# Six gate chunks moved into an earlier decode stage, dilated softmax sums taken from the exponentials and swapped as turned rows, and half of the experts' down projection split into high and low parts

## The chip, the cores and the metric

The kernel runs on one core of one Trainium2 chip. The metric is device time in microseconds (us) of one launch; three runs of the kernel before gave 2228.87, 2231.35 and 2236.27 us, median 2231.35 us.

## The reference, cut to what matters

One layer of a decoder for 1024 prompt tokens and 8 sample tokens (one for each of 8 sequences with 256 cached positions), model width 1024, fp32:

```
u = rmsnorm(h);  z = u @ W_in          # q,k,v of 12 dilated and 8 stick-breaking heads, gates g_a and g_b
h += ( sigmoid(g_a) * (dilated(u) @ W_oa) + sigmoid(g_b) * (stick(u) @ W_ob) ) @ W_out
h += experts(rmsnorm(h))               # 32 experts, 2 for each token: (silu(x @ Wg) * (x @ Wu)) @ Wd
h += sigmoid(rmsnorm(h) @ W_pg) * (p @ W_pp);   y = rmsnorm(h)
```

Dilated attention has three groups of four heads: windows 128, 512 and 2048 with strides 1, 4 and 16. The three groups of one head position are joined by a softmax over their log-sums, which is one softmax over all their keys: all exponentials take one common maximum for each query and are divided by one common sum. Stick-breaking attention takes a reverse running sum of softplus over the keys. For the sample tokens both kinds read cached keys and values (the stick-breaking ones from pages named by a table).

## The kernel before, in words

The kernel is a chain of stages, each a block that all engines enter and leave together: norm and projection, `stick_and_gates` (L368), `dilated` (L672), `decode` (L970), merge, residual, routing, `experts` (L1761), finish.

Matmuls that go by `products` (L83 to L89) split both fp32 operands into a high part (a ScalarE copy to fp32r) and a low part (a VectorE subtraction) and make three one-pass products: high by low, low by high, high by high. Other matmuls are plain fp32; the trace has two instructions for each.

`stick_and_gates`: 64 units (4 head pairs, 8 query tiles in the order 7,0,6,1,5,2,4,3, 2 heads) go through a pipeline written out by hand: step s scores one part (ScalarE copies it out), masks unit s-1, exponentiates s-2, scans s-3 (VectorE), s-4 exponentials, turns s-5 on TensorE, s-6 values, s-7 out. Between these TensorE is given matmuls of the two output gates, shared out evenly over the steps: 16 chunks of 128 columns, each 3 groups of 344 tokens by 24 products, 1152 in all (`gates`, L545). Each chunk is loaded by SP (L474), split by ScalarE (L569) and VectorE (L626), and goes out to DRAM as `gT`.

`dilated`: two head pairs. A pair has 16 units of 128 queries: units 0 to 7 are the stride-1 group with natural rows of queries, units 8 to 15 the other two groups with queries in classes modulo 4. Scores run 18 steps ahead of the exponentials (between the pairs 4 more steps), since the maxima of the two orders have to be joined: SP writes the maxima of units 0 to 7 to DRAM element by element (L795), reads them back by classes (L798), writes those of units 8 to 15 (L801) and reads them back in natural order (L804); VectorE joins them (L927, L929). Then for each unit: exponential (ScalarE L900), turn on TensorE (L843) and copies out (ScalarE L893, VectorE L935), values (TensorE L867) twice, once with V and once with a tile of ones, which gives the sums, and eviction of both (ScalarE L886 for units 0 to 7, VectorE L960 adds for 8 to 15). At the end of a pair VectorE takes the reciprocal of 128x1024 sums (L964) and multiplies (L966).

`decode`: scores of the 8 sample tokens on VectorE (multiply and reduce over loaded keys, L1153, L1177, L1181), softmax or the stick-breaking chain on 32 or 64 rows, then values: a row of all heads is made (L1260, L1266), masked to each head's own columns on VectorE (L1199, L1203) and turned by products with ones (L1274). The pages of keys and then of values go into one buffer (`KV` is `big`), so the value pages are loaded only after all key products (L1070). TensorE has nothing else to do in this stage.

`experts`: 32 blocks of 128 rows, two for each pass of a loop, software-pipelined: in a step TensorE makes the gate of block n-1, turns the hidden rows of n-2, makes up of n-1, turns the rows of n, and makes down of n-2 (L1891, plain fp32, 4 parts of the hidden width by 2 halves of the output). ScalarE order: output of n-3, sigmoid of n-1, high parts of Wg, x, Wu of n. VectorE order: gated n-1, copy of the turned hidden rows n-2, low parts of Wg, hidden n-1, low parts of x and Wu. Each block loads 6 MB of weights and 0.5 MB of rows and stores 0.5 MB.

Of the kernel before, what the change touches and what calls it, by code (L numbers as in the profile page):

```python
# [19 lines left out]
P = 128  # L20
D = 1024
# [30 lines left out]
NEG = -1.0e30  # L52
SCALE = HD ** -0.5
# [314 lines left out]
def stick_and_gates(nc, g):  # L368
# [5 lines left out]
    with ctx:  # L374
# [10 lines left out]
        CH = 2 * KD  # L385
# [12 lines left out]
        gw = sb("g_w", [P, KD, P])  # L398
        gwh = sb("g_wh", [P, 2, KD, P], F32R)
        gwl = sb("g_wl", [P, 2, KD, P], F32R)  # L400
# [4 lines left out]
        acc = [ps(f"g_acc{j}", [P, 512]) for j in range(2)]  # L405
# [6 lines left out]
        gw_in = sem("g_w_in")  # L412
        g_out = [sem(f"g_g_out{j}") for j in range(2)]
        gwh_full, gwl_full, acc_full, gate_full = map(sem, ("g_wh_full", "g_wl_full", "g_acc_full", "g_gate_full"))
# [48 lines left out]
        def _(sp):  # L463
# [8 lines left out]
            def load_gate(c):  # L472
                need(sp, gwl_full, c)
                sp.dma_start(gw[:, :, :], win_v[:, :, QKV + c * P:QKV + (c + 1) * P]).then_inc(gw_in, 16)  # L474
# [7 lines left out]
            for s in range(LAST + 1):  # L482
# [8 lines left out]
                for c in range(CH):  # L491
                    if evict_at[c * NSPLIT + NSPLIT - 1] == s:
                        sp.wait_ge(gate_full, (c + 1) * NSPLIT)
                        sp.dma_start(gT[c, :, :], gate[:, c % 2, :]).then_inc(g_out[c % 2], 16)
            for b in range(2):
                sp.wait_ge(g_out[b], 16 * CH // 2)
# [175 lines left out]
def dilated(nc, g):  # L672
# [6 lines left out]
    with ctx:  # L679
# [12 lines left out]
        EXP_LAG, TURN_LAG, VALUE_LAG, EVICT_LAG = 18, 19, 20, 21  # L692
# [24 lines left out]
        def keys(u, x, m):  # L717
# [9 lines left out]
        LAST = max(at_evict) + 1  # L727
# [7 lines left out]
        acc = sb("acc", [P, PAIRS, 2, SEQ])  # L735
        ones = sb("ones", [P, HD])
        mst = sb("mst", [P, PAIRS, 2, UNITS])
        oth = sb("oth", [P, PAIRS, 2, UNITS])
        nm = sb("nm", [P, PAIRS, 2, UNITS])
# [6 lines left out]
        O = [ps(f"O{n}", [P, 512]) for n in range(2)]  # L746
        drawn, kept, bias_step, bias_set = map(sem, ("drawn", "kept", "bias_step", "bias_set"))
        s_full, row_full, joint_step, nm_full, p_full, tp_full, o_full, oa_read, ob_read, fin = map(sem, (
            "s_full", "row_full", "joint_step", "nm_full", "p_full", "tp_full", "o_full", "oa_read",
            "ob_read", "fin"))  # L750
        pT_full = [sem(f"pT_full{b}") for b in range(2)]
# [3 lines left out]
        m_in = [sem(f"m_in{p_}") for p_ in range(PAIRS)]  # L755
# [4 lines left out]
        def nat(p_, n):  # L760
            return maxes[p_, n, :, :].rearrange("b (i p) -> p b i", p=P)
# [4 lines left out]
        by_class = lambda t, p_: t[:, p_, :, QT:UNITS].rearrange("p b (h r) -> p b h r", h=2)  # L766

        @block.sync
        def _(sp):
            def load_qk(p_, x):  # L770
                c = x * PAIRS + p_
# [1620 lines left out]
```

## Time and profile before

| what | value |
|---|---|
| median of three runs | 2231.35 us |
| the profiled execution: device time, span | 2228.89 us, 2227.3 us |
| TensorE busy, VectorE, ScalarE, GpSimd | 1855.4, 1057.1, 800.7, 128.4 us |
| mean granted TensorE clock | 0.911 |
| DMA moved | 401.73 MB, mean 180 GB/s |
| stick_and_gates | 443 to 787 us |
| dilated | 787 to 984.6 us |
| decode | 984.6 to 1108 us |
| experts | 1403 to 2041 us |

The span is the time from the first to the last instruction; the device time of the same execution lies 1.6 us above it. Busy shares are of the whole span; what counts is the stage. A granted clock of 1.00 is 2.4 GHz and 0.50 is 1.2 GHz.

### The profile page before, as it was taken

How to read it: one execution, taken by the hardware profiler on the slowest of the kernel's cores; microseconds unless marked ns; L12 is line 12 of the kernel's file. 1: busy time of each engine (PE TensorE's matmuls, PEld its weight loads, DVE VectorE, ACT ScalarE, POOL GpSimd, SP SyncE). 2: the span in 40 equal slices, each digit the busy share in tenths (PEclk: the TensorE clock that was granted, in tenths of full speed). 3: DMA queues.
4: the chain of work that ended last, by engine and by line, in shares of the span. 5: the costliest groups of instructions: out<-in, count | busy, mean ns of one | idle time of the engine just before them, and what ended most of it. 6: DMA issues, size and time to landing. Idle time of an engine off the chain costs nothing. (4 is left out here: it accounts for less than half of the span.)

```text
span 2227.3 us, 26881 instructions
## 1 busy us (share of the span) xinstructions
PE 1855.4 (83%) x9852; PEld 1443.3 (65%) x9852; DVE 1057.1 (47%) x1415; ACT 800.7 (36%) x1096; POOL 128.4 (6%) x181
## 2 busy tenths in 40 slices
PE   5999999789999947632498992599999999996698
PEld 4999999777777835431295541466666677773585
DVE  5211211158888733335151224466666666662674
ACT  4111111147666503220040000454555555452454
POOL 0111111100000000010031003000000000001110
PEclk7999999989999978675699995699999999998799
DMA  3443444245221160025354213899999999994620
GB/s 114 116 121 114 131 126 122 92 140 172 67 86 39 39 180 1 1 55 152 99 167 145 76 39 137 354 390 379 381 384 385 382 385 382 382 378 164 224 75 39
DMA packets 165325, 401.73 MB, mean 180 GB/s; under 512 B 25659, under 2 KB 102955, under 8 KB 144772
## 3 DMA queue, kind: packets, MB, share of 16 engines
q1 hardware_dynamic: 146004, 334.32, 41.8%
q0 software_dynamic: 10320, 33.82, 5.3%
q10 hardware_dynamic: 8928, 32.63, 3.6%
q8 instruction: 45, 0.74, 0.1%
q14 instruction: 28, 0.23, 0.0%
HBM read 325.80 MB, written 82.61 MB: 183 GB/s over the span
## 5 line engine op out<-in xcount | busy, mean ns | idle before, releaser
L87 PE MATMUL p_acc<-uh,p_wl 128*128 128x344 f32 x720 | 234.9, 326 | 13.0 <-DVE ul L293 9.0
L89 PE MATMUL p_acc<-uh,p_wh 128*128 128x344 f32 x720 | 230.6, 320 | 0.0
L88 PE MATMUL p_acc<-ul,p_wh 128*128 128x344 f32 x720 | 230.5, 320 | 0.0
L1891 PE MATMUL x_Y<-x_wd,x_hT 128*128 128x512 f32 x512 | 225.1, 593 | 0.8 <-DVE x_hT L1989 0.8
L305 DVE COPY p_zk<-p_tp 128x512 f32<-128x512 f32 (+1 forms) x90 | 44.2, 547 | 304.4 <-PE p_tp L226 304.4
L1973 DVE TENSOR_TENSOR x_wgl<-x_wg,x_wgh 128x2048 fp32r<-128x2048 f32 x64 | 143.9, 2290 | 49.8 <-ACT x_wgh L1930 49.8
L1891 PEld LDWEIGHTS x_Y<-x_wd,x_hT 128*128 128x128 f32 x512 | 95.0, 190 | 108.2 <-issue 107.1
L269 ACT ACTIVATE p_zc<-p_acc 128x344 f32<-128x344 f32 x90 | 41.2, 458 | 321.6 <-PE p_acc L89 321.6
L1973 DVE TENSOR_TENSOR x_wul<-x_wu,x_wuh 128x2048 fp32r<-128x2048 f32 x64 | 143.8, 2289 | 17.8 <-ACT x_wuh L1930 17.8
L87 PEld LDWEIGHTS p_acc<-uh,p_wl 128*128 128x128 f32 x720 | 135.8, 189 | 18.0 <-issue 14.9
L545 PE MATMUL g_acc<-uh,g_wl 128*128 128x344 f32 x384 | 129.1, 336 | 9.3 <-ACT u L576 7.1
L89 PEld LDWEIGHTS p_acc<-uh,p_wh 128*128 128x128 f32 x720 | 136.0, 189 | 0.0
L88 PEld LDWEIGHTS p_acc<-ul,p_wh 128*128 128x128 f32 x720 | 135.8, 189 | 0.0
L1930 ACT ACTIVATE x_wgh<-x_wg 128x2048 fp32r<-128x2048 f32 x64 | 118.8, 1905 | 47.2 <-DMA x_wg<-in_w_gate 47.2
L1505 PE MATMUL r_acc<-r_w,mT 128*128 128x512 f32 (+1 forms) x288 | 127.3, 601 | 10.1 <-DMA r_w<-in_w_out 10.1
L545 PE MATMUL g_acc<-ul,g_wh 128*128 128x344 f32 x384 | 127.4, 332 | 0.0
L545 PE MATMUL g_acc<-uh,g_wh 128*128 128x344 f32 x384 | 126.9, 330 | 0.0
L87 PE MATMUL x_G<-x_wgh,x_xl 128*128 128x512 f32 x256 | 114.0, 445 | 11.5 <-DVE x_xl L1967 11.5
L1930 ACT ACTIVATE x_wuh<-x_wu 128x2048 fp32r<-128x2048 f32 x64 | 118.5, 1901 | 0.3 <-DMA x_wu<-in_w_up 0.3
L1978 DVE TENSOR_TENSOR x_gs<-x_sg,x_G 128x512 f32<-128x512 f32 x32 | 22.1, 689 | 178.6 <-ACT x_sg L1923 178.6
L1505 PEld LDWEIGHTS r_acc<-r_w,mT 128*128 128x128 f32 (+1 forms) x288 | 51.6, 182 | 79.6 <-issue 69.2
L87 PE MATMUL x_U<-x_wuh,x_xl 128*128 128x512 f32 x256 | 102.9, 402 | 0.0
(316 smaller groups left out, 3676.8 us busy)
## 6 DMA issues: line engine op xcount, KB each, us to landing
x_wg<-in_w_gate SPq DMA_DIRECT2D x64, 1024.0 KB, 7.7
x_wu<-in_w_up SPq DMA_DIRECT2D x64, 1024.0 KB, 7.4
x_wd<-in_w_down SPq DMA_DIRECT2D x32, 2048.0 KB, 12.5
x_x<-xs SPq DMA_DIRECT2D x32, 512.0 KB, 11.6
ys<-x_y ACTq DMA_DIRECT2D x32, 512.0 KB, 11.8
zT<-p_zc ACTq DMA_DIRECT2D x30, 516.0 KB, 3.4
p_w<-in_w_in SPq DMA_DIRECT2D x30, 512.0 KB, 5.5
ztok<-p_zk POOLq DMA_DIRECT2D x30, 512.0 KB, 4.6
```

The costliest lines, as they stand in the source:

```text
L87: pe.matmul(out, w_low, m_high, start=first, stop=False)
L88: pe.matmul(out, w_high, m_low, start=False, stop=False)
L89: return pe.matmul(out, w_high, m_high, start=False, stop=last)
L269: act.activation(zc[:, b, s * NS:(s + 1) * NS], acc[b * NSPLIT + s][:, 0:NS], ACT.Copy).then_inc(zc_full, 1)
L305: dve.tensor_copy(zk[0:r, b, t0:t0 + m, :], tp[j % 2][0:r, 0:m, :]).then_inc(zk_full, 1)
L545: last = pe.matmul(acc[grp % 2][:, 0:NS], lhs[:, c % 2, kk, :], rhs[:, kk, t], start=(x == 0), stop=(x == M - 1), skip_group_check=True)
L1505: last = pe.matmul(acc[t % 2][0:r, c * 512:(c + 1) * 512], mT[:, k, t * P:t * P + r], w[:, k, c * 512:(c + 1) * 512], start=(k == 0), stop ...
L1891: last = pe.matmul(Y[c][:, :], hT[:, k, :], wd[:, b, k, c * 512:(c + 1) * 512], start=(k == 0), stop=(k == KF - 1))
L1930: act.activation(wh[:, HALVES[half], :], w[:, HALVES[half], :], ACT.Copy).then_inc(full, 1)
L1973: dve.tensor_tensor(wl[:, s, :], w[:, s, :], wh[:, s, :], ALU.subtract).then_inc(full, 1)
L1978: dve.tensor_tensor(gs[:, :], sg[:, :], G[:, :], ALU.mult).then_inc(gs_full, 1)
```

## The change

1. `decode` becomes `decode_and_gates` and runs before `stick_and_gates`. Its TensorE program has 20 steps, and in 18 of them it makes one group (24 products) of the first 6 gate chunks, the decode work standing ahead of the group in its step. The gate loads are issued by ScalarE. Key pages get a buffer of their own; value pages share the buffer of the dilated keys and queries and wait for `scored`. Values are made turned at once: V or the value page is the stationary operand and the weights of all heads the moving one, and a mask and a sum (`own_heads`) keep each head's own rows.
2. `stick_and_gates` makes the other 10 chunks (720 products), shared out over the same steps.
3. `dilated` drops the products with ones. Each exponential gives its row sums (`accum_out`). Maxima and sums change order as rows: natural ones are turned on TensorE to 16 rows of 128 and written in one piece. The natural maxima leave during the scoring. After the last exponential of a pair the class sums go by DRAM to natural rows, are turned and added, the reciprocal is taken of 128x16 values, turned, written, and read back broadcast to all partitions. The loads of V and of the second pair's q and k are issued by ScalarE.
4. `experts` splits two of the four hidden parts of the down projection into high and low parts (ScalarE and VectorE) and makes three products of each; the other two stay plain fp32.

The core of the diff:

```diff
+DECODE_GATES = 6
-            stick_and_gates(nc, g)
+            decode_and_gates(nc, g, DECODE_GATES)
+            stick_and_gates(nc, g, DECODE_GATES)
...
             dilated(nc, g)
-            decode(nc, g)
@@ stick_and_gates
-        CH = 2 * KD
+        CH = 2 * KD - c0
@@ dilated, TensorE
-                for side in range(2):
-                    for n, (x, t) in enumerate(tiles):
-                        for b in range(2):
-                            left = ones[:, :] if side else v[:, p_, x, t, h]
+                for n, (x, t) in enumerate(tiles):
+                    for b in range(2):
+                        last = pe.matmul(O[a % 2][h, 0:P], v[:, p_, x, t, h], pT[:, a % 2, b, n * P:(n + 1) * P], ...)
@@ dilated, ScalarE
+            act.wait_ge(qk_in[0][1], 32)
+            load_v(act, 0)
+            for x in range(N_DIL):
+                load_qk(act, 1, x)
+            load_v(act, 1)
...
-                        act.activation(r, r, ACT.Exp, scale=SCALE, bias=nm[:, p_, b, u:u + 1]).then_inc(p_full, 1)
+                        act.activation(r, r, ACT.Exp, scale=SCALE, bias=one(nm, p_, b, u),
+                                       accum_out=one(den, p_, b, u)).then_inc(p_full, 1)
@@ dilated, SP
+                for p_ in range(PAIRS):
+                    natural_out(p_)
+                    sp.wait_ge(row_full, 2 * (p_ + 1) * UNITS)
+                    classes_out(p_, mst, 1, mrows[:, p_, 1, :], m_out[p_][1], m_in[p_][1])
+                for p_ in range(PAIRS):
+                    sp.wait_ge(p_full, 2 * (p_ + 1) * UNITS)
+                    classes_out(p_, den, 2, drows[:, p_, 0, :], n_out[p_][0], n_in[p_][0])
+                    sp.wait_ge(inv_kept, p_ + 1)
+                    sp.dma_start(natural(p_, 3), drows[:, p_, 1, :]).then_inc(n_out[p_][1], 16)
+                    sp.wait_ge(n_out[p_][1], 16)
+                    for b in range(2):
+                        sp.dma_start(inv[b * HD:(b + 1) * HD, p_, :], maxes[p_, 3, b, :]...broadcast_to([HD, SEQ]))
@@ decode_and_gates
+        D_SCORES_T, D_PROBS_T, D_VALUES = 6, 7, 8
+        S_SCORES_T, S_WEIGHTS_T, S_VALUES = 13, 14, 16
+        STEPS = GROUPS + 2
+        S_SCORES = {9: (0, 1), 10: (1, 3), 11: (3, 5), 12: (5, 8)}
+        cut_at = {max(0, (c - 1) * NSPLIT): c for c in range(1, chunks)}
...
+            def outputs_T(o, rows_, weights, heads, b0, b1):
+                for b in range(b0, b1):
+                    for c in range(o.shape[1]):
+                        for x in range(2):
+                            last = pe.matmul(o[:, c, b, :], rows_(x, b)[:, c * P:(c + 1) * P],
+                                             weights[:, x, b * heads:(b + 1) * heads], ...)
@@ experts
             def down(n, b, it):
+                    if k < KS:
+                        pe.wait_ge(dl_full, n * KS + (k + 1))
...
+                        if k < KS:
+                            last = products(pe, Y[c][:, :], hh[:, k, :], hl[:, k, :], wdh[:, k, cols], wdl[:, k, cols],
+                                            k == 0, False)
@@ experts, ScalarE step
                 if three:
                     output(*three)
+                if two:
+                    high_down(*two)
                 if one:
                     sigmoid(one[0])
+                if two:
+                    high_hidden(two[0])
@@ experts, VectorE step
+                if two:
+                    low_down(two[0], two[1])
                 if one:
                     gated(one[0])
@@ experts, ScalarE end
                 output(last - 1, 0, np_ - 1)
+                high_down(last, 1, np_ - 1)
+                high_hidden(last)
                 output(last, 1, np_ - 1)
```

## Rows read from the trace of the kernel before

**Rows 1.** Windows, by stage: start:end, us, busy by engine, granted clock, DMA share, GB/s
```profile
443.00:787.00 344.00, 308.98 (x2208) 257.95 (x2208) 257.57 (x432) 208.50 (x385) 0.49 (x2) 0.98 0.28 91
787.00:984.60 197.60, 122.13 (x972) 91.14 (x972) 70.88 (x201) 46.72 (x112) 2.24 (x7) 0.73 0.18 49
984.60:1108.00 123.40, 43.24 (x168) 23.68 (x168) 40.79 (x55) 3.60 (x7) 10.41 (x32) 0.61 0.46 127
1403.00:2041.00 638.00, 619.83 (x2432) 432.94 (x2432) 387.16 (x256) 318.66 (x257) 0.00 (x0) 0.98 0.94 367
```

**Rows 2.** Windows inside stick_and_gates
```profile
475.00:755.00 280.00, 260.52 (x1881) 214.63 (x1882) 234.71 (x397) 185.49 (x346) 0.00 (x0) 1.00 0.28 90
595.00:635.00 40.00, 34.99 (x251) 28.32 (x249) 34.56 (x58) 25.61 (x48) 0.00 (x0) 1.00 0.15 53
```

**Rows 3.** Timeline of stick_and_gates (start us, us): gate products, early and later
```profile
456.25 0.49 PE L545 MATMUL g_acc<-uh,g_wh 128*128 128x344 f32 x1
...
600.05 0.32 PE L545 MATMUL g_acc<-uh,g_wl 128*128 128x344 f32 x1
600.21 0.32 PE L545 MATMUL g_acc<-ul,g_wh 128*128 128x344 f32 x1
```

**Rows 4.** Groups by line, 450 to 783 us: busy, mean ns, idle before
```profile
L626 DVE TENSOR_TENSOR g_wl<-g_w,g_wh 128x1024 fp32r<-128x1024 f32 x16 | 19.6, 1223 | 43.5 <-ACT g_wh L569 43.5
```

**Rows 5.** Groups by line and form, dilated
```profile
L867 PE MATMUL d_O<-d_pT,d_ones 128*64 128x128 f32 x312 | 31.3, 338 | 0.0
```

**Rows 6.** Timeline of dilated, from the last scores of pair 0 to its first exponential
```profile
811.51 3.80 SPq L795 DMA_DIRECT2D maxes<-d_mst  x2
812.52 0.68 DVE L952 CUSTOM_DVE_ANT_0 d_row<-d_bias,d_S 128x512 f32<-128x512 f32 x1
824.83 0.87 SPq L798 DMA_DIRECT2D d_oth<-maxes  x2
825.75 0.98 SPq L801 DMA_DIRECT2D maxes<-d_mst  x2
831.46 0.19 DVE L927 TENSOR_TENSOR d_oth<-d_oth,d_mst 128x32 f32<-128x32 f32 x1 [18.25 <-DMA d_oth<-maxes]
```

**Rows 7.** Timeline of dilated, between the pairs and at the end
```profile
913.10 6.55 DVE L964 RECIPROCAL d_acc<-d_acc 128x1024 f32<-128x1024 f32 x1
...
969.43 1.32 ACT L900 ACTIVATE d_row<-d_row,d_nm 128x512 f32<-128x512 f32 x2
983.13 1.22 DVE L966 TENSOR_TENSOR u<-d_acc 128x1024 f32<-128x1024 f32 x1
```

**Rows 8.** Window inside dilated
```profile
930.00:940.00 10.00, 8.52 (x58) 6.39 (x54) 1.27 (x3) 3.55 (x11) 0.00 (x0) 0.50 0.00 0
```

**Rows 9.** Timeline of decode: first scores, one of 8 key products, last products
```profile
1006.48 2.29 DVE L1153 TENSOR_TENSOR g_big<-g_big 128x2048 f32<-128x2048 f32 x1 [22.13 <-DMA g_big<-ztok]
1057.11 1.22 DVE L1177 TENSOR_TENSOR g_big<-g_big,e_wide 128x1024 f32<-128x1024 f32 x1
1058.36 1.28 DVE L1181 TENSOR_REDUCE e_s<-g_big 128x8 f32<-128x512 f32 x2
1097.00 10.03 PE L1274 MATMUL e_bank<-c_ones,e_wide 8*128 8x1 f32 x64 [0.77 <-DVE e_wide L1203]
```

**Rows 10.** Window inside experts
```profile
1580.00:1680.00 100.00, 100.00 (x401) 70.09 (x400) 64.11 (x44) 50.91 (x43) 0.00 (x0) 1.00 0.97 384
```

**Rows 11.** Timeline of experts: every third gate product, then the last down projections
```profile
1708.84 0.39 PE L87 MATMUL x_G<-x_wgh,x_xl 128*128 128x512 f32 x1
...
1709.52 0.39 PE L87 MATMUL x_G<-x_wgh,x_xl 128*128 128x512 f32 x1
...
2023.37 7.03 PE L1891 MATMUL x_Y<-x_wd,x_hT 128*128 128x512 f32 x16
2030.23 0.63 PE L1882 MATMUL x_tph<-ident,x_hm 128*128 128x128 f32 x4
```

**Rows 12.** DMA issues of the page: count, KB each, us to landing
```profile
x_wd<-in_w_down SPq DMA_DIRECT2D x32, 2048.0 KB, 12.5
```

More of the change, by code:

```diff
@@ L844, in turn, with evicted, bank_read, bank_free @@
                     last.then_inc(tp_full, 1)
-            def values(a):
+            def evicted(a):
+                e_, w = place(a)
+                if w < QT:
+                    pe.wait_ge(oa_read, e_ * QT + w + 1)
+                else:
+                    pe.wait_ge(ob_read, e_ * QT + w - QT + 1)
+            def bank_read(s):
+                for steps, done, per in ((at_nat, nat_kept, 1), (at_joint, joint_step, 2), (at_sum, total_step, 2),
+                                         (at_inv, inv_kept, 1)):
+                    need(pe, done, per * sum(t < s for t in steps))
+            def bank_free(s):
+                before = [a for t, a in at_value.items() if t <= s and a % 2 == 0]
+                if before:
+                    evicted(max(before))
+                bank_read(s)
+            def values(a, at_step):
                 p_, u = place(a)
@@ L1133, in _ @@
                 keep(bias[:, 1, h:h + 1], True, OWN + N_DIL, -NEG)
-            then(pool.memset(ones[:, :], 1.0))
-            then(pool.memset(head[:, :, :], 0.0))
-            then(pool.affine_select(out=head[:, :, :], in_=head[:, :, :], compare_op=ALU.not_equal, fill=1.0,
-                                    base=0, pattern=[[-1, H_B], [0, HD]], channel_multiplier=1))
+            then(pool.memset(own[:, :, :], 0.0))
+            for c in range(CB):
+                for half in range(2):
+                    then(pool.memset(own[half * HD:(half + 1) * HD, c, 2 * c + half:2 * c + half + 1], 1.0))
             pool.memset(mx[:, :], 0.0).then_inc(bias_set, 1)
@@ L1171, in dilated_softmax, with own_heads @@
                 dve.tensor_scalar(st[:, :, :], st[:, :, :], mx[:, 3:4], None, ALU.mult).then_inc(pn_full, 1)
+            def own_heads(dst, src, full, heads):
+                dve.wait_ge(full, 1)
+                n = src.shape[1]
+                m = masked[:, 0:n * DEC * heads].rearrange("p (c b h) -> p c b h", c=n, b=DEC)
+                for c in range(n):
+                    ins = dve.tensor_tensor(m[:, c, :, :], src[:, c, :, :],
+                                            own[:, c, 0:heads].unsqueeze(1).to_broadcast([P, DEC, heads]), ALU.mult)
+                    if c < n - 1:
+                        ins.then_inc(dve_step, 1)
+                        steps[0] += 1
+                    else:
+                        then(ins)
+                dve.tensor_reduce(dst, m, AX, ALU.add).then_inc(done, 1)
             def stick_scores(b):
@@ L1280, in _ @@
+            for n in range(STEPS):
+                if n == D_SCORES_T:
                     pe.wait_ge(s_full, 2)
@@ L1941, in step @@
             def step(it, j):
-                one, three = lag(it, j, 1), lag(it, j, 3)
+                one, two, three = lag(it, j, 1), lag(it, j, 2), lag(it, j, 3)
                 new = it * 2 + j
```

587 lines of the change are left out of this document (343 added, 244 removed).

## The prediction

> **What bounds the kernel now.** I began with the windows by stage [rows 1]. Nearly all of the change falls into four stages: stick_and_gates, 344 us; dilated, 198; decode, 123; experts, 638. The reader is to see that each has a limit of its own. In stick_and_gates TensorE is busy 309 of 344 us at a clock of 0.98. In decode it is busy 43 of 123, the hole into which work is moved. In dilated it is busy 122 of 198 at a mean clock of 0.73, and DMA stands still. In experts it is busy without a break in the steady part, while DMA is 0.97 busy [rows 10]. Then I looked inside the stages. In the steady part of stick_and_gates TensorE has 260.5 of 280 us and VectorE 234.7 [rows 2]: TensorE ends last, but VectorE is only a tenth behind. The timeline of dilated shows two holes made by the join of the maxima [rows 6, 7] and steps in which TensorE alternates between values, sums and turns [rows 5]. The timelines of decode and experts give the chains below [rows 9, 11].
>
> **1. stick_and_gates loses 6 of 16 chunks.** That is 6 x 72 = 432 products. At full clock one starts every 0.158 us [rows 3], so TensorE loses 68.3 us of work. VectorE loses 6 splits of 1.22 us [rows 4], 7.3 us, ScalarE less than 15 us, and it is not the bound at 185 of 280 us [rows 2]. In the 280 us window TensorE's share of the loss is about 58 us, so its need falls to 203, and VectorE's to 229: VectorE is late next. The stage can't win 68 us. Before, VectorE stood idle 45 us in this window. Its largest wait in the whole stage, 43.5 us for the high part of a gate chunk [rows 4], is partly the start, which stays; the rest of its waits come from TensorE being late and mostly go. Bounds for the window: no idle left, 229 (a gain of 51); all of it left, 274 (a gain of 6). I take 15 us of idle, 244, a gain of 36, since TensorE now has 40 us to spare and the pipeline lets it run about a step ahead, but the heavy and light units alternate. Behind the last unit, after the window, fewer products fill TensorE: 6 us more, bounds 0 and 8. Together -42 us, bounds -6 and -59.
>
> **2. decode takes the 6 chunks in.** TensorE's own time: the first gate product can't come earlier than in stick_and_gates, some 13 us after that stage began [rows 1, 3], since gate loads, both splits and table loads are the same; 18 groups, 68.3 us; values as 32 + 64 matmuls of two instructions, 192, at the 0.157 us of the old turned outputs, whose stationary side has the same 128 columns [rows 9], 30 us; turns and the end, 5 us. Sum 116, and with nothing late that is the lower bound less what warmer clock gives on the values, 108. What can be late: the scores of step 6 need keys and queries, which before were there 22 us after the stage began [rows 1, 9] and now share the DMA queues with the gate loads, the broadcast queries of the stick-breaking heads and the first pages. Take 30; VectorE then needs 4 x 2.3 us for both scores, 39, and TensorE would be at step 6 at 13 + 23 = 36: a stall of 3 to 5 us. The second: VectorE's split of chunk 4 stands ahead of the first key product of a page and waits for step 8 of TensorE, about 60; from there 8 sequences at 2.5 us [rows 9], 20 us, and two splits, 2.4, give 83, while TensorE reaches step 13 at about 75: 8 us. These two bring 116 to 128; the values at full clock give some 5 back: 123 us. The old stage took 123.4 [rows 1], so the edit comes out at 0. Bounds: 108 (-15) and, with keys 10 us later still and the value pages late by 5, 138 (+15). SP's queue holds keys, queries, pages, V, pages and value pages in one order; decode's 15.7 MB (127 GB/s x 123.4 us) and six gate loads of 0.5 MB, 19 MB, need 160 GB/s of DMA that is 0.46 busy at 127 [rows 1]: not the bound.
>
> **3. dilated.** (a) The first hole. The last scores of pair 0 end at 813.2; the join, on which the exponentials wait, comes at 831.5 [rows 6]. Of this 11.6 us are behind the element-wise write of natural maxima (issued 811.5, done 824.8). It leaves during scoring now. What stays is one round trip, 825.75 to 831.46, 5.7 us, plus a turn and one more VectorE instruction, 0.8: join at 819.7, gain 12 us. If the row write queues behind V loads until 818, 5 us less; the bounds are 7 and 13. (b) The second hole: the reciprocal at 913.1 takes 6.55 us, the multiplication behind it 1.2, the join 0.4, and only at 921.3 can an exponential start [rows 7]. The reciprocal goes, but the same round trip from 913 with the turn ends at 919: 2 us won, bounds 0 and 5. (c) The products with ones: 312 instructions, 31.3 us of TensorE [rows 5]. The step's chain is values, sums, turn, copies, so they are on it; four fifths pass through, 25 us (bounds half and all). Against it each of 64 exponentials reads an accumulator; no row shows it; the smallest VectorE instruction shown takes 0.19 us [rows 6], 12 us for all, mostly hidden behind TensorE: 3 us, bounds 0 and 12. (d) Less dense TensorE work makes a lower clock likely. 122.1 - 31.3 = 90.8 us of its work remain at a mean clock of 0.73 [rows 1]; at 0.69 they take 5 us more, which I take; bounds -13 (0.85) and +42 (0.50). (e) The end. Before, from the last exponentials at 970.75 to 984.35 were 13.6 us with values, reciprocal and multiplication [rows 7]. Now: two round trips of the size of the one in [rows 6], each 5.7 with two turns and four small VectorE steps, 3; broadcast load of 0.5 MB 1 us longer; multiplication 1.2: 16 us, +2, bounds -1 and +6. Waits inside the steps for the shared bank are put at 0: sums of pair 0 are taken in steps of pair 1 in which the evictions named are a step old. (f) The maxima of pair 1 and its loads now stand on ScalarE and SP while these are idle: 0. Sum of dilated: -12 - 2 - 25 + 3 + 5 + 2 = -29; all lower ends together are -63, all upper ones +37.
>
> TensorE shows 0.50 in 930 to 940 with 8.5 of 10 us busy [rows 8], so in this stage busy time alone does not hold the clock. The Trainium skill (TensorE: Matmul & The Clock Gate, Part 4: PE-mode transpose) says that transposes do not count as busy in the way of other matmuls. By that rule the change, which removes only non-transposes, leaves the stage colder; the trace agrees as far as that window goes.
>
> **4. experts.** The down projection of a block is 16 fp32 instructions, 6.86 us from 2023.37 to 2030.23, 0.429 each [rows 11]. Eight of them become 12 products at 0.227 (three in 0.68 [rows 11]): 3.43 becomes 2.72, 0.7 us for each block, 22 us for 32 if TensorE stays the bound. But a block moves 7.32 MB (367 GB/s x 638 us / 32 [rows 1]); at 384 GB/s with DMA 0.97 busy [rows 10] it takes 19.1 us, and at 396, all of DMA busy, 18.5: at most 18 us can be won, and queues this full seldom give their last per cent. I take 14, 2/3 of TensorE's 22; bounds 0 and 20. ScalarE gets two copies of 1024 columns at some 1.3 us (it passes as many columns as two of 512 in 1.32 [rows 7]) and one of 256 for each block, VectorE two subtractions of 1.22 [rows 4] and one small: they go from 51 and 64 of 100 us to 67 and 78 [rows 10], no bound. On ScalarE the copy of Wd stands ahead of the sigmoid and waits for the down weights: behind it queue sigmoid, Wg, x, Wu, and on them all of TensorE. The weights are issued behind the down projection that frees their buffer, one step, 19 us, ahead of this copy, and took 12.5 [rows 12], so the wait is 0, with 6 us to spare. At the end the last down projection can't be prepared under the one before, as the buffer is single: eviction 1.3, two copies 2.6 at most, hidden rows 0.4, VectorE 1.5 behind it, against a turn of 0.63 [rows 11] and one copy: +4, bounds +3 and +6. Sum -10, bounds -17 and +6.
>
> The DMA rate shown is 384 GB/s [rows 10]. The Trainium skill (DMA: Bandwidth & Descriptors, Specifications) gives some 358 GB/s as the limit of HBM for one core. By that rule the stage would be bound by DMA already and win nothing; the trace lies above the figure, so it doesn't settle it.
>
> **The sum.** -42 + 0 - 29 - 10 = -81. The profiled execution took 2228.9 us (span 2227.3), which gives 2148. It lies 2.4 us under the median of the three runs, so 2150. A move of 0.3%, 6.7 us, is about what a measurement of this kernel tells from none.
>
> **The rivals.**
> A. Dilated stays at 1.2 GHz after the removal. For it: [rows 8]. Against: the mean of the stage is 0.73 [rows 1] with the same turns. Price: +42 in place of +5, time 2187.
> B. Experts is held by DMA: no gain, the end costs 4: +14, time 2164. For it: DMA 0.97 busy in every steady stretch. Against: TensorE shows no gap in the window, so it waited for no DMA there.
> C. All passes through: stick_and_gates -54, decode -12, dilated -38, experts -16: 2228.9 - 120 + 2.4 = 2111. For it: the stages are separate; against: VectorE at 229 of any shorter window [rows 2].
> D. Slower: in stick_and_gates TensorE, now waiting for VectorE in every step, falls to 1.2 GHz. Its work left, 309 - 68 = 241 us [rows 1], would take 482 against the 302 that I give the stage: 180 us times the cold share of the stage, and from a share of 0.45 the whole gain is eaten; with 0.6 of it cold the time is 2258. At 1.2 GHz a gate product takes 0.49 us in place of 0.32 [rows 3]. Against it: from 595 to 635 TensorE was busy 0.87 of the time, about what is to come, at a clock of 1.00 [rows 2].
> E. The change doesn't do what it says: the moved groups don't fit beside decode, and the stage grows by more than 15 us. TensorE idled 80 us there [rows 1] against 68 moved, so the ordered steps would have to stall 27 us and not 12. It is counted with A's chance, at about the same time.
>
> **How the numbers follow.** The forecast, 2125 to 2165 around 2150: 0.50. B: 0.16. A or E: 0.14. C: 0.14. D: 0.06. The likeliest is the forecast. The bounds of the four stages taken together reach from 2077 to 2283, but they don't fall on one side at once; 2105 to 2190 takes in B, A and a part of what lies around C. Faster by over 0.3%: 0.93; within: 0.02; slower: 0.05, nearly all of it D.
>
> **What would show it.** In stick_and_gates VectorE over 0.9 busy in the steady part, the stage about 300 us long at a clock near 1. decode_and_gates between 115 and 135 us with waits of TensorE at steps 6 and 13. In dilated a first hole of 7 us, a second of 6, widest steps about 1 us shorter, and an end of 16 us behind the last exponential. In experts a period between 18.5 and 18.9 us in place of 19.1. The prediction is wrong if the waits in decode_and_gates exceed 20 us, if VectorE keeps its idle time in stick_and_gates, or if the clock of a stage falls by over 0.1.

## The result and the profile after

The changed kernel takes 2177.01 us (median of 4 runs, 2173.68 to 2179.61), the kernel before 2230.11 beside it: a ratio of 0.9761 with an interval of 0.9728 to 0.9795, 53 us less. The forecast was 2150, its range 2105 to 2190. The profiled execution took 2174.56 us (span 2172.8, clock 0.906), so it lies 2.4 us under its median, as the one of before did.

The windows by stage answer to [rows 1]. Here the decode stage comes first; a stage begins with the first load that SyncE issues for it, experts with its first gate product.

```profile
443.20:595.30 152.10, 112.82 (x632) 111.03 (x632) 40.93 (x55) 17.66 (x32) 11.19 (x39) 0.77 0.50 145
595.30:899.20 303.90, 251.07 (x1776) 199.15 (x1776) 248.87 (x426) 195.19 (x361) 0.47 (x2) 0.93 0.25 82
899.20:1067.40 168.20, 109.53 (x668) 74.53 (x668) 56.27 (x209) 50.82 (x176) 2.16 (x6) 0.68 0.21 64
1376.50:1987.20 610.70, 597.13 (x2552) 455.78 (x2552) 458.77 (x349) 384.83 (x349) 0.00 (x0) 0.99 0.94 376
```

| stage | before | after | difference | forecast |
|---|---|---|---|---|
| decode | 123.4 | 152.1 | +28.7 | 0 |
| stick_and_gates | 343.9 | 303.9 | -40.0 | -42 |
| dilated | 197.7 | 168.2 | -29.5 | -29 |
| experts, from the first gate product | 626.5 | 610.7 | -15.8 | -10 |

The four add up to -56.6, the span lost 54.5. Three stages lie within the bounds that the prediction gave them (experts with 6 us more than its forecast). The decode stage, bounded at +15, doesn't; there 29 us of the expected gain went.

**Inside the decode stage.** The waits from 443 to 592 us (who waited, for whom: us in total, times, longest) show what TensorE stood for behind its start:

```profile
PE g_acc L88 <- DVE g_wl L1256: 17.6, 1, 17.6
PE e_bank L1433 <- DVE u L1304: 9.0, 1, 9.0
PE g_acc L88 <- ACT u L1358: 8.3, 2, 5.4
PE c_bank L1424 <- DVE u L1280: 7.5, 1, 7.5
```

The first line is the start. The others are 24.8 us: 8.3 before groups 3 and 6, whose gate chunks came late (the wait is put down to ScalarE's eviction L1358, which is queued behind the split of the late chunk), 7.5 at step 7 for the softmax, 9.0 at step 13 for the key products. VectorE's timeline shows why the last two are so long:

```profile
487.67 1.22 DVE L1256 TENSOR_TENSOR g_wl<-g_w,g_wh 128x1024 fp32r<-128x1024 f32 x1 [5.56 <-ACT g_wh L1348]
499.58 1.23 DVE L1256 TENSOR_TENSOR g_wl<-g_w,g_wh 128x1024 fp32r<-128x1024 f32 x1 [10.69 <-ACT g_wh L1348]
500.73 0.41 DVE L1275 COPY u<-c_bank 32x256 f32<-32x256 f32 x1
...
518.34 0.22 DVE L1294 TENSOR_REDUCE u<-u 128x16 f32<-128x64 f32 x1
525.58 1.23 DVE L1256 TENSOR_TENSOR g_wl<-g_w,g_wh 128x1024 fp32r<-128x1024 f32 x1 [7.02 <-ACT g_wh L1348]
526.72 1.22 DVE L1300 TENSOR_TENSOR e_pk<-e_pk,e_wide 128x1024 f32<-128x1024 f32 x1
...
546.23 1.28 DVE L1304 TENSOR_REDUCE u<-e_pk 128x8 f32<-128x512 f32 x2
```

The softmax's first copy (L1275) could start at 487, when its turned scores were there, but stands behind the split of chunk 3, for which VectorE waits 10.7 us. All 24 key instructions (8 products, 16 sums) stand behind the split of chunk 4, which waits for group 8; the last ends at 547.5.

Why the chunks are late shows in the DMA columns of three windows of the stage, of which the mean, 0.50, shows nothing:

```profile
446.00:509.00 63.00, 39.22 (x195) 38.31 (x196) 15.85 (x16) 7.70 (x14) 8.38 (x37) 0.73 1.06 300
464.00:470.00 6.00, 4.30 (x28) 4.02 (x26) 0.00 (x0) 0.00 (x0) 0.00 (x0) 1.00 1.14 167
509.00:595.00 86.00, 73.60 (x439) 72.73 (x437) 25.08 (x39) 8.88 (x17) 0.00 (x0) 0.80 0.09 33
```

For 63 us the DMA engines have no time to spare (1.06), then hardly any work (0.09); and from 464 to 470 us they are as full with 167 GB/s as elsewhere with 300. Chunk 1 takes 16.3 us from its issue to its split on ScalarE, chunk 2 takes 13.9, chunk 3 takes 9.6.

The value products come in three stretches of 64. The windows of the first stretch, of the group behind it, and of the second stretch with the start of its group show TensorE busy without a gap, and its mean clock under 1.00:

```profile
509.20:518.00 8.80, 8.80 (x67) 8.80 (x66) 0.00 (x0) 0.46 (x1) 0.00 (x0) 0.81 0.02 9
518.00:523.50 5.50, 5.50 (x26) 5.50 (x27) 0.51 (x3) 0.00 (x0) 0.00 (x0) 0.68 0.00 0
561.60:573.70 12.10, 12.10 (x74) 12.10 (x73) 0.00 (x0) 0.46 (x1) 0.00 (x0) 0.68 0.00 0
```

Each of these clocks is a mean of both levels: the first stretch has 1.00 up to 513.5 us and 0.50 from 515. A group of 24 gate products ends 3.9 us behind its start at full clock. Eight of the 18 took 5.5 to 6.8 us: group 0, the four behind a wait (3, 6, 7, 13) and the three behind values (8, 16, 17).

**The other three stages.** In dilated the first hole is what the forecast said: the last scores end at 925.5, the class maxima go out at 925.6, are asked for again as rows 4.5 us later, turned at 931.75, and the first exponential starts at 932.46. The second hole, from the last maximum (1000.7) to the next exponential (1006.0), is 5.3 us. The last line is the cost that no row of before showed, the reading of a row sum: 0.19 us each, 12.2 for 64.

```profile
925.62 0.88 SPq L816 DMA_DIRECT2D maxes<-d_mst  x2
930.15 0.32 SPq L818 DMA_DIRECT2D d_mrows<-maxes  x1
931.75 0.25 PE L921 MATMUL d_O<-ident,d_mrows 16*128 16x16 f32 x1 [7.49 <-DMA d_mrows<-maxes]
932.46 0.40 ACT L976 ACTIVATE d_row<-d_row,d_nm 128x128 f32<-128x128 f32 x1 [37.19 <-DVE d_nm L1009]
932.76 0.19 ACT L976 ACTIVATION_READ_ACCUMULATOR d_row<-d_row,d_nm 128x1 f32 x1
```

Windows inside stick_and_gates (answers to [rows 2]) and experts (answers to [rows 10]):

```profile
635.00:880.00 245.00, 206.97 (x1514) 161.88 (x1515) 226.43 (x394) 173.35 (x325) 0.00 (x0) 0.96 0.22 72
...
1600.00:1700.00 100.00, 100.00 (x436) 77.03 (x435) 78.38 (x61) 67.03 (x61) 0.00 (x0) 1.00 0.99 395
```

VectorE is now 0.92 busy in stick_and_gates and TensorE 0.84. In experts TensorE is still without a gap and the period fell from 19.2 to 18.5 us, by TensorE's whole 0.7. Its end shows a new wait:

```profile
1966.08 0.63 PE L2022 MATMUL x_tph<-ident,x_hm 128*128 128x128 f32 x4
...
1968.60 2.00 ACT L2083 ACTIVATE x_wdh<-x_wd 128x1024 fp32r<-128x1024 f32 x2 [1.23 <-issue]
1969.69 2.36 DVE L2161 TENSOR_TENSOR x_wdl<-x_wd,x_wdh 128x1024 fp32r<-128x1024 f32 x2 [8.87 <-ACT x_wdh L2083]
...
1972.77 0.80 PE L88 MATMUL x_Y<-x_wdh,x_hl 128*128 128x512 f32 x1 [6.05 <-DVE x_hl L2156]
```

### The profile page after: what moved, and what is told of

Its sections match the earlier page's. It is cut to its first block and busy times, and to the rows that moved or that the text cites. A ratio compares the mean times of both kernels' runs of the same rounds, so it can differ in the third digit from the quotient of the medians.

```text
span 2172.8 us, 27019 instructions
## 1 busy us (share of the span) xinstructions
PE 1834.6 (84%) x9708; PEld 1480.1 (68%) x9708; DVE 1111.3 (51%) x1513; ACT 878.6 (40%) x1256; POOL 129.1 (6%) x186
## 5 line engine op out<-in xcount | busy, mean ns | idle before, releaser
L2138 DVE TENSOR_TENSOR x_wgl<-x_wg,x_wgh 128x2048 fp32r<-128x2048 f32 x64 | 143.9, 2290 | 54.5 <-ACT x_wgh L2077 54.5
L88 PE MATMUL x_G<-x_wgh,x_xl 128*128 128x512 f32 x256 | 113.0, 441 | 10.8 <-DVE x_xl L2132 10.8
L2038 PE MATMUL x_Y<-x_wd,x_hT 128*128 128x512 f32 x256 | 115.5, 594 | 0.0
L2161 DVE TENSOR_TENSOR x_wdl<-x_wd,x_wdh 128x1024 fp32r<-128x1024 f32 x64 | 75.5, 1222 | 77.5 <-ACT x_wdh L2083 77.5
L89 PE MATMUL x_G<-x_wgl,x_xh 128*128 128x512 f32 x256 | 100.7, 393 | 0.0
L90 PE MATMUL x_G<-x_wgh,x_xh 128*128 128x512 f32 x256 | 100.7, 393 | 0.0
L90 PE MATMUL x_U<-x_wuh,x_xh 128*128 128x512 f32 x256 | 100.4, 392 | 0.0
L89 PE MATMUL x_U<-x_wul,x_xh 128*128 128x512 f32 x256 | 99.7, 390 | 0.0
## 6 DMA issues: line engine op xcount, KB each, us to landing
x_wd<-in_w_down SPq DMA_DIRECT2D x32, 2048.0 KB, 12.6
ys<-x_y ACTq DMA_DIRECT2D x32, 512.0 KB, 10.7
```

The lines of the kernel that those rows point to most:

```text
L88: pe.matmul(out, w_low, m_high, start=first, stop=False)
L89: pe.matmul(out, w_high, m_low, start=False, stop=False)
L90: return pe.matmul(out, w_high, m_high, start=False, stop=last)
L2038: last = pe.matmul(Y[c][:, :], hT[:, k - KS, :], wd[:, b, k, cols], start=False, stop=(k == KF - 1))
L2138: dve.tensor_tensor(wl[:, s, :], w[:, s, :], wh[:, s, :], ALU.subtract).then_inc(full, 1)
L2161: dve.tensor_tensor(wdl[:, k, :], wd[:, b, k, :], wdh[:, k, :], ALU.subtract).then_inc(dl_full, 1)
```

## The experiments

All ratios are to the kernel before on the same chip; the changed kernel stands at 0.9761. A difference between two kernels is taken from their ratios, 0.001 being 2.2 us, and is no surer than their intervals; stage times come from the profiled execution of each.

### The parts alone

Each is the kernel before with one part of the diff (for the first, `decode` and the gates of `stick_and_gates` by the new functions; for the others the new `dilated` or `experts` alone).

> The kernel before with only the decode and stick-breaking part of the change (six gate chunks in the decode stage); dilated attention and experts as before. Theory: the parts add up, and each stage's loss or gain in the trace of the changed kernel is its own: decode stage +28.7 us, stick-breaking -40.3, so the kernel is 11 to 12 us faster than before (ratio about 0.995). Rival: the decode stage's loss comes partly from neighbours (transfers that the next stages issue earlier), or the prediction's sum (-42 + 0) holds here and something else in the changed kernel costs it: then -35 to -42 us (ratio 0.983).

> The kernel before with only the dilated-attention part of the change. Theory: the dilated stage goes from 197.7 to about 168 us by itself, -29 to -30 us on the whole (ratio 0.987). Rival: part of the stage's gain in the changed kernel comes from what stands before it (the clock with which stick-breaking hands over, no transfers left over), then -20 to -25 us here.

> The kernel before with only the experts' half-split hidden rows. Theory: TensorE is the bound of the block period, 26 periods lose 0.70 us each (18 us) and the last block's end gives 2 to 4 back: -14 to -16 us (ratio 0.993). Rival: transfers carry part of the period, then -8 us or less.

Measured: 0.9963 (0.9940 to 0.9986), 0.9899 (0.9857 to 0.9941), 0.9922 (0.9895 to 0.9949). They sum to -0.0216 against the whole's -0.0239, within the intervals: the parts add up. The stages are those of the whole change: stick-breaking 303.7 us, dilated with decode behind it 292.1 us against 321.2 (-29.1), experts from first load to next stage 626.0 against 641.3 (-15.3). The loss in the decode stage belongs to the first part alone. There it measured 158.8 us, not 152.1, with nearly the same waits (25.7 us for 24.8) and colder values: the 64 dilated value products took 11.6 us instead of 8.7. Two later runs with the decode stage unchanged gave 158.1 and 158.7. So 152 is the short end of what this stage takes, in the main by clock. For dilated the ratio of the whole kernel (-22.5 us) would suit its rival; its interval takes in both, and it is the stage itself that speaks for the theory. That stage, too, differs between executions: with the same instructions it took 164.2 to 172.4 us in the profiles of the changed kernel and nine later runs, at clocks of 0.71 to 0.64.

### How many chunks belong there

```diff
-DECODE_GATES = 6
+DECODE_GATES = 8     # gates8
+DECODE_GATES = 5     # gates5, with STEPS = max(GROUPS, 16) + 2
```

> The changed kernel with eight gate chunks in the decode stage instead of six, so eight and not ten behind it in stick-breaking. Theory: stick-breaking beside six chunks fewer is already bound by VectorE's chain with TensorE just behind, so two more chunks moved give it 10 us or less, while the decode stage grows by six groups of 3.7 to 5.3 us (22 to 30 us): 12 to 22 us slower than the changed kernel, 2189 to 2199 us. Rival: TensorE still carries stick-breaking's period, which then falls by the two chunks' whole 22 us: within 5 us of the changed kernel.

> The changed kernel with five gate chunks in the decode stage and eleven behind it in stick-breaking. Stick-breaking gave back only 2.6 us for chunks 7 and 8. Theory (VectorE's chain is its bound with six chunks out, and still with five): stick-breaking +1 to +4 us, the decode stage -11 to -14 us: 7 to 12 us faster than the changed kernel. Rival (TensorE becomes its bound again just at five): stick-breaking +11 us for the chunk, 0 to 3 us in all; or the decode stage's own chain ends last once three groups are gone, and it shrinks by less than 6 us.

Measured: gates8 0.9873 (0.9839 to 0.9907), 2200.67 us, 24 more than the changed kernel; gates5 0.9767 (0.9730 to 0.9804), 2176.60 us. With eight chunks the decode stage took 181.2 us (+29.1) and stick-breaking 301.3 (-2.6), although 22 us of TensorE work left it: theory right for both stages, while the whole came out a little over its 12 to 22 us. (Some 6 of the 29 us are colder values again: 32.4 us for the three stretches, 26.7 in the changed kernel.) With five, decode 138.0 (-14.1) and stick-breaking 314.4 (+10.5), the chunk's whole TensorE time: there the rival was right. The windows of stick-breaking's steady part, gates8 first:

```profile
664.00:905.00 241.00, 192.05 (x1379) 145.15 (x1380) 221.35 (x389) 169.13 (x316) 0.00 (x0) 0.94 0.19 62
```

```profile
620.00:870.00 250.00, 215.12 (x1557) 169.74 (x1555) 223.38 (x389) 174.40 (x326) 0.00 (x0) 0.95 0.23 75
```

VectorE has 0.92 of gates8's window and 0.89 of gates5's, TensorE 0.80 and 0.86. The limit passes from TensorE to VectorE's chain between five and six chunks; six is where a moved chunk stops giving its 11 us.

### The late weights

```diff
+    first_w = gate[:, 1, 0:D]           # chunk 1's raw weights, still free here
     load_gate(0)
+    load_gate(1)
...
-    if c + 1 < chunks: load_gate(c + 1)
+    if c != 1 and c + 1 < chunks: load_gate(max(2, c + 1))
```

> The changed kernel with gate chunk 1's raw weights loaded at the decode stage's start, right behind chunk 0's, into the (still free) second row of the gates' output tile; chunk 2's load then follows chunk 0's split, so that both are asked for some 16 to 19 us before today. Theory: the loads issued at 453.96 and 472.64 come late behind SyncE's queue of cache pages, and their lateness makes the waits before groups 3 and 6 (5.4 and 2.9 us), the cold starts of these groups (1.6 us each) and, through the split that stands in ScalarE's and VectorE's order, part of the 7.5 us at step 7: decode stage 152 to between 139 and 144 us, the kernel 8 to 13 us faster than the changed one. Rival: the transfers as a whole (270 GB/s in this stretch) are the limit, and the earlier gate loads only push the pages back: 3 us or less.

Measured 0.9753 (0.9719 to 0.9787), no change that can be told: the rival's result. The theory's mechanism showed, its gain didn't. The wait before group 3 went (5.4 to 0), group 6 started at 482.7 instead of 490.0, but the softmax was held by the split of chunk 3 all the same, as VectorE's timeline shows:

```profile
480.44 1.22 DVE L1259 TENSOR_TENSOR g_wl<-g_w,g_wh 128x1024 fp32r<-128x1024 f32 x1
494.12 1.23 DVE L1259 TENSOR_TENSOR g_wl<-g_w,g_wh 128x1024 fp32r<-128x1024 f32 x1 [12.45 <-ACT g_wh L1351]
495.26 0.41 DVE L1278 COPY u<-c_bank 32x256 f32<-32x256 f32 x1
```

Step 7's wait was 9.4 us instead of 7.5, step 13's again 9.0, and two of the three stretches of values took 3 us longer at a lower clock. The stage was 153.5 us. The DMA share from 446 to 503 us was 1.07: the earlier loads met the same full queues. Chunk 3, issued 7.2 us earlier than in the changed kernel, reached its split 5.5 us earlier.

```diff
     sp.wait_ge(table_in, 16)
+    sp.wait_ge(kq_in, 12 * 16)
     for b in range(2): ... load_page(PK, b, x, 0, ek_in[b])
```

> The changed kernel with the key pages and the values of the cache asked for only when the dilated keys and queries have landed, so that gate chunk 1 (issued 453.96) meets less in the queues. Theory (traffic ahead of it makes chunk 1 late): chunk 1 lands 4 to 8 us earlier and the wait of 5.4 us before group 3 goes; 4 to 10 us faster than the changed kernel, as long as the pages still come before step 9's key products. Rival (the pages take the same 0.5 MB pieces' time whenever they are asked for, and VectorE's chain sets the waits at steps 7 and 13): within 3 us, or slower by what the last pages come later.

Measured 0.9737 (0.9700 to 0.9773); the stage took 152.6 us. Chunk 1 was split at 469.8 instead of 471.4, the wait before group 3 stayed at 5.3 us: the pages were not what made it late. The windows show what else was ahead of it:

```profile
446.00:467.00 21.00, 13.36 (x72) 13.08 (x72) 1.23 (x1) 1.06 (x1) 8.08 (x37) 0.73 1.09 293
467.00:472.00 5.00, 0.00 (x0) 0.00 (x0) 2.20 (x2) 1.56 (x3) 0.00 (x0) 0.90 0.03 4
```

The keys, the queries and the copies of the queries to all partitions, all issued before chunk 1 or within 6 us behind it, keep the DMA engines full to 467 us, and ScalarE can split chunk 1 at 468.7. Chunk 2, issued at 471.1 into nearly empty queues, is there for its split 4.4 us later, where it took 13.9 in the changed kernel. So traffic does make the weights late, as the theory said, but other traffic than it named, and its 4 to 10 us did not come. That the keys and queries are the cause for chunk 1 is read from these times; no run took them away. (VectorE split chunk 2 at 480.4 instead of 487.7, so that the wait before group 6 went, and step 7's fell to 6.1; step 13's stayed at 9.0, and the dilated values took 11.6 us for 8.7.)

### The cold values

```diff
     for kk in range(KD):
         last = products(pe, acc[grp % 3], ...)
+        if beside: beside(kk)      # values of one sequence, in steps 8, 16 and 17
```

> The changed kernel with the value products put between the gate products of the same step (the dilated values of one sequence behind each of group 8's eight sets of three products, a stick-breaking sequence behind every second set of groups 16 and 17) instead of in one stretch ahead of them. Theory (the granted clock falls to 1.2 GHz in the stretches of 64 value products, 0.81 and then 0.68 behind them, though TensorE is busy without a gap): groups 8, 16 and 17, which take 5.34, 5.83 and 5.49 us instead of 3.7, start at full clock, and the kernel is 4 to 6 us faster than the changed one. Rival (what lowers the clock is the wait ahead of the values, or mixing lowers it for the whole step): within 1.5 us of it, or slower.

Measured 0.9770 (0.9736 to 0.9803), the stage 154.8 us. The two mixed stretches:

```profile
508.20:524.00 15.80, 15.80 (x90) 15.80 (x89) 0.10 (x1) 1.57 (x3) 0.00 (x0) 0.67 0.07 26
561.20:593.00 31.80, 31.80 (x164) 31.80 (x163) 0.00 (x0) 0.92 (x3) 0.00 (x0) 0.61 0.00 1
```

Theory wrong: put between gate products, the values take the clock of the whole step down with them (0.67 and 0.61, TensorE busy throughout). They keep the lower clock near them wherever they stand. Whether one stretch harms less is not shown: the values and their groups took 15.4 and 34.8 us mixed, 14.1 and 29.9 in the changed kernel's profile, but 33.1 for the second place in part_decode, plain_last and split4, and 34.7 in the combined run, all with whole stretches.

### The order in VectorE's queue

```diff
-S_SCORES = {9: (0, 1), 10: (1, 3), 11: (3, 5), 12: (5, 8)}
+S_SCORES = {7: (0, 4), 8: (4, 6), 9: (6, 7), 10: (7, 8)}
 # vector
-    if n in cut_at: cut(cut_at[n])
+    if n in cut_at and n != D_SCORES_T: cut(cut_at[n])
     if n == D_PROBS_T: dve.tensor_copy(pT, pT_ps)
+                       cut(cut_at[D_SCORES_T])
 # scalar: the exponential of step 6 ahead of cut(3)
```

> The changed kernel with only the order inside VectorE's and ScalarE's queues changed in the decode stage: the dilated softmax stands before the split of gate chunk 3 instead of behind it (on both engines), and the key products of stick-breaking stand at steps 7 to 10 (four sequences right behind the copy of the probabilities) instead of 9 to 12. Nothing is added or left out. Theory (the added waits are the place of the vector work in the queue: the softmax waits behind a split that waits for weights, and 22 us of key products wait behind the split of chunk 4, which waits for group 8's last product, so that TensorE waits 9.0 us at step 13 in every variant so far, whatever was gained before it): the waits of 7.5 and 9.0 us and one or two cold starts go, decode stage 152 to between 132 and 140 us, the kernel 12 to 20 us faster than the changed one (2157 to 2165 us). Rival (the clock gives back what the waits lose, as with the earlier weights, or the waits come back behind the splits): less than 6 us.

Measured 0.9684 (0.9650 to 0.9719), 2156.48 us: 17 us less than the changed kernel, within what theory gave, with the same instructions. The stage took 132.0 us. Its windows from end to end, and VectorE's timeline:

```profile
443.20:575.20 132.00, 107.84 (x632) 106.41 (x632) 40.94 (x55) 17.53 (x31) 11.13 (x39) 0.82 0.58 167
```

```profile
489.91 0.41 DVE L1275 COPY u<-c_bank 32x256 f32<-32x256 f32 x1
...
501.64 1.23 DVE L1256 TENSOR_TENSOR g_wl<-g_w,g_wh 128x1024 fp32r<-128x1024 f32 x1 [4.76 <-ACT g_wh L1349]
502.78 1.22 DVE L1300 TENSOR_TENSOR e_pk<-e_pk,e_wide 128x1024 f32<-128x1024 f32 x1
...
523.21 1.28 DVE L1304 TENSOR_REDUCE u<-e_pk 128x8 f32<-128x512 f32 x2
```

VectorE is busy 40.9 us, as in the changed kernel. The softmax comes 10.8 us earlier and the key products end at 524.5 instead of 547.5, before TensorE asks for them at 531; the waits at steps 7 and 13 are gone. Groups 7 and 13 start warm (4.1 and 4.0 us for 6.1 and 6.0), and the mean clock rises from 0.77 to 0.82. The theory's "9.0 us in every variant so far" was not quite so (6.9 in mix, 7.9 in gates5), and the run does not part the softmax's place from that of the key products.

It also answers what mix left open, whether a wait ahead of the values lowers their clock. Here TensorE works at full clock for 26 us with no wait, and the clock falls in the values all the same:

```profile
517.00:543.00 26.00, 26.00 (x168) 25.68 (x166) 10.15 (x15) 6.48 (x12) 0.00 (x0) 1.00 0.22 82
543.20:551.70 8.50, 8.50 (x65) 8.50 (x64) 0.00 (x0) 0.46 (x1) 0.00 (x0) 0.82 0.00 0
```

### The experts' down projection

```diff
-KS = KF // 2
+KS = KF            # all four hidden chunks split, no plain products
```

> The changed kernel with all four hidden chunks of an expert block split (three quick products each) instead of two split and two plain. Theory (TensorE is still the bound of the 18.52 us period, the transfers next at 18.3 to 18.5 us): its 0.7 us per block go, but the period falls by 0.2 us or less: 0 to 6 us faster than the changed kernel. Rival (the transfers, now at 0.99 to 1.00 of their share, still follow the pace of TensorE, since they are asked for by it): the period falls by the whole 0.7 us to 17.8, 16 to 19 us faster. A third way: VectorE and ScalarE, which get two more splits per block, make it longer.

Measured 0.9718 (0.9677 to 0.9759), 2162.61 us, 10 us less than the changed kernel although its decode stage was one of the long ones (158.7 us). Experts itself took 603.7 us against 624.6, both from first load to next stage: 21 us less. The rival was right in the stage; the ratio alone, with its interval, would suit either. A window inside:

```profile
1600.00:1700.00 100.00, 100.00 (x477) 83.82 (x476) 92.88 (x70) 80.66 (x74) 0.00 (x0) 1.00 1.01 413
```

The period is 17.77 us. The transfers follow TensorE to 413 GB/s; a DMA share of 0.97 or 0.99 was the pace at which they were asked for, not their limit. The Trainium skill (DMA: Bandwidth & Descriptors, Specifications) gives some 358 GB/s of HBM for one core; the trace, in which one core works alone, does not agree, and the measurement decides.

```diff
-    down(last, 1, np_ - 1)                  # split: high, low, hidden rows
+    down_plain(last, 1, np_ - 1)            # 16 plain fp32 products from one copy, hlast
```

> The changed kernel, in which the last expert block's down product is made plain in fp32 from one copy of the hidden rows, without split and without their low half. Theory (the half split costs the last block a chain that nothing covers: the split on ScalarE and VectorE between the turned hidden rows and the first product, 6.05 us of waiting against 0.8 before, and a cold start behind it): 5 to 7 us faster than the changed kernel, all of it after the last gate product. Rival (a plain product takes four times the passes at either clock, and eats what the wait gives back): within 2 us.

Measured 0.9767 (0.9736 to 0.9798) for the whole: no difference. But its decode stage was a long one (158.1 us against 152.1), and the place itself shows the gain: 617.2 us for experts against 624.6, 7.4 less.

```profile
1973.67 0.69 DVE L2196 COPY x_hlast<-x_tph 128x512 f32<-128x512 f32 x1 [5.93 <-PE x_tph L2023]
...
1974.43 7.12 PE L2049 MATMUL x_Y<-x_wd,x_hlast 128*128 128x512 f32 x16 [0.80 <-DVE x_hlast L2196]
```

The wait is 0.8 us for 6.05, and the projection stays at full clock: 7.1 us for 9.4. Of the whole kernel's time that is argued from the stage, not shown by the ratio.

### All of it

> The version that the runs point to: the changed kernel with the order of the reorder run, the earlier loads of gate chunks 1 and 2 of the prefetch run, all four hidden chunks split as in the split4 run, and the last down product plain as in the plain_last run. Theory (four separate causes, which add up now that VectorE's late key products no longer set step 13): 2156 us of the reorder run, less 18 to 21 us in the experts' periods, 5 to 7 us at their end, 5 to 9 us for the waits of 5.7 and 4.1 us before groups 3 and 6 and their cold starts: 2120 to 2130 us, a ratio to the kernel before of 0.952 to 0.957. Rival (the earlier loads give nothing here either, since the clock or the pages take it back): 2128 to 2138 us.

Measured 2120.53 us (2118.78 to 2125.19), ratio 0.9499 (0.9475 to 0.9522): by the ratios 58 us less than the changed kernel. The time lies at the lower end of the theory's range, the ratio just under its 0.952 to 0.957. Decode 130.4 us, stick-breaking 304.2, dilated 168.9, experts 594.8 from first load. Experts has 30 of it (21 and 7, as alone; the rest is that with four chunks split the wait at the end, 8.3 us in the split4 run, went too) and decode 22 (28 against the long ones). The earlier weights took the wait before group 3 away again and brought group 7 from 496.5 to 488.4, but of these 8 us the stage gave only 1.6: the values behind it ran colder once more (10.8 and 11.1 us for the last two stretches, 8.7 and 9.1 in the reorder run), and groups 8, 16 and 17 took 3.3 us longer.

## Why the prediction was right in kind and 27 us short

- **stick_and_gates, -42: right** (-40.0). VectorE had 0.92 of the steady part, TensorE waits for it there at the values, 30 times and 37.2 us in all, and gates8 shows it directly. Rival D, the fall to 1.2 GHz, didn't come: 0.93 over the stage.
- **decode, 0: wrong, and the failed step is TensorE's own time, "18 groups, 68.3 us".** It took every moved product at the full clock that [rows 3] shows inside a dense stage, though the early product of the same rows, at 0.49 us, shows a cold start. Here the groups took 84 us, 16 more. Four groups ran cold for a part behind a wait and three behind value products, where TensorE was never idle; group 0 did at the stage's start. Next to it, the waits: I had 12 us at two places. They measured 16.5: the second was seen rightly in place and cause, the first came at step 7 and not at 6, by the split of chunk 3 and not by late keys. The two for late gate chunks, 8.3, were not seen at all: the loads were counted as bytes over the whole stage (160 GB/s, "not the bound"), but the DMA engines are full from 446 to 509 us. The sign that the prediction set for itself, waits over 20 us in this stage, came true with 24.8. With 2 us more for the values and 2 less for the start: 16 + 12.8 + 2 - 2 = 29, the whole difference in this stage. (The kernel missed by 27 us: the other three stages together gave 4 us more than forecast, the rest of the kernel took 2 us longer.) The reorder run shows that 20 us of it hang on the place of two pieces of vector work in VectorE's queue: what the forecast called the edit's own waits was the order's.
- **dilated, -29: right** (-29.5), by terms that partly offset. The first hole is 7 us, as forecast. The end behind the last exponential is 13.9 us, where I said 16. TensorE's clock is 0.68 where I said 0.69. But its busy time fell by 12.6 us (122.1 to 109.5), not by the 26 that (c) and (d) give before their discount: the value products and turns that stayed became longer (means of 337 to 374 and 337 to 375 ns), and TensorE's idle time fell by 17 us instead. And that the sum came out within half a microsecond is luck, in a stage that differs by up to 8 us between executions. The Trainium skill (TensorE: Matmul & The Clock Gate, Part 4: PE-mode transpose) holds that turns don't count as other matmuls do, by which the stage had to become colder; the trace agrees, 0.73 to 0.68 (0.64 to 0.71 in the other runs), though the value products of the decode stage, which aren't turns, did the same. Whether the row sums' 12.2 us on ScalarE cost anything was not tried.
- **experts, -10: right in sign, its discount wrong.** I took 14 of TensorE's 22 us for fear of the transfers; all passed (0.7 us in each period), and split4 shows another 0.7 free behind it. For "queues this full seldom give their last per cent" there was no row; the share went to 0.99 and in split4 to 1.01, with 413 GB/s where I had 396 for all of DMA busy. The end cost 7 us by the plain_last run, I had said 4 and left out the cold start behind the wait.
- **Rivals.** B is refuted by split4, C by the decode stage, A and D by the clocks. E is what happened, at its own price: it named stalls of 27 us as the point from which the stage grows by 15; the waits were 24.8, and the clock did the rest. I had counted it with A and given it no sum of its own; 2177 us lies outside the 2125 to 2165 to which I had given 0.50.

## What to carry to other kernels

When matmuls are moved from a dense stage into the holes of a sparse one, cost them at the clock that the sparse stage will have: here each of the host stage's waits (2.9 to 9.0 us) made the group behind it 1.6 to 2.1 us longer. Then look at what stands ahead of the urgent vector work in its queue; a split that waits for a weight buffer is a bad neighbour for a softmax, and here a change of order alone gave 17 us where earlier loads gave none that can be told. And look at the DMA share window by window: a mean of 0.50 held 63 us at 1.06 in which weights of 0.5 MB took 10 to 16 us. A busy DMA share just under 1 beside a TensorE without gaps says who sets the pace only if one of the two is changed: take work from TensorE and see.

## What was not expected of the hardware

- Matmuls with 4 or 8 moving columns lower the granted clock while TensorE is busy all the time: 0.81 and 0.68 in and behind a stretch of 64, 0.61 to 0.67 when mixed with gate products of 344 columns. In the reorder run the fall came with no wait ahead of it.
- One execution differs from the next by up to 6 us in the decode stage and 8 us in dilated, with the same instructions, in the main by the clock (8.7 to 11.6 us for the same 64 value products). A profile of one execution can be the lucky one: in plain_last a gain of 7.4 us in experts stood beside a decode stage 6.0 us longer, and the two spans differ by 1 us.
- DMA moved 413 to 417 GB/s in the steady part of experts once TensorE asked for it, 384 before.
- From 464 to 470 us of the decode stage the DMA engines were as full (1.14) with 167 GB/s as in other windows with 300 to 400.
- Reading the row sum of an exponential took 0.19 us on ScalarE, behind each of the 64.
